# The ends of four layers: both products taken in two passes of 512 columns over the rows, with the gate weights split in between

## The reference

```
h = h + mixer(...) @ w_out            # block 2: h + rms_norm(mixer @ w_out, post_gain)
gate = sigmoid(h @ ple_gate[i])       # 1024 x 1024 weights
h = h + gate * (p[i] @ ple_proj[i])   # side input p: 1024 x 256
...
hn = rms_norm(h, next_gain)           # before the next layer
```

## Time and profile before

| | |
|---|---|
| median of three runs | 4260.09 us (4253.25, 4260.09, 4288.84) |
| profiled execution | 4255.36 us |
| its span | 4253.6 us |
| PE busy | 3758.1 us, 88% of the span |
| VectorE (DVE) busy | 2016.2 us, 47% |
| ScalarE (ACT) busy | 1703.1 us, 40% |
| DMA | 265.62 MB, mean 62 GB/s |
| landing of a 512 KB load of old h, median | 7.8 us after its issue |
| mean granted clock of TensorE | 0.91 of full speed |

### The profile page before, as it was taken

One profiled execution on the slowest core, in us unless ns is written; L12 is line 12 of the kernel. 1 busy time (PEld: TensorE's weight loads), 2 busy tenths in 40 slices (PEclk: granted clock), 3 DMA queues, 4 the chain that ended last, 5 costly groups with the idle time before them and its releaser, 6 DMA issues. The chain is left out here.

```text
span 4253.6 us, 48223 instructions
## 1 busy us (share of the span) xinstructions
PE 3758.1 (88%) x18866; PEld 3044.6 (72%) x18866; DVE 2016.2 (47%) x3934; ACT 1703.1 (40%) x3132; POOL 107.6 (3%) x120
## 2 busy tenths in 40 slices
PE   6999679889995999999788999999788999998789
PEld 5888337668883777777666777777676688877666
DVE  3143323354335667775334455555544355565441
ACT  3222461344332333342234444444433465655420
POOL 0011120000000000000000000000000000000000
PEclk9999799989995777788899999999898999999789
DMA  3333302212222121121321111010122111110310
GB/s 125 114 127 114 111 0 80 85 45 94 103 76 74 40 63 40 40 50 40 124 79 41 33 31 31 26 36 21 45 90 80 63 32 40 35 35 11 134 50 40
DMA packets 219642, 265.62 MB, mean 62 GB/s; under 512 B 62620, under 2 KB 142612, under 8 KB 218392
## 3 DMA queue, kind: packets, MB, share of 16 engines
q1 hardware_dynamic: 219416, 262.53, 18.9%
HBM read 191.95 MB, written 70.52 MB: 62 GB/s over the span
## 5 line engine op out<-in xcount | busy, mean ns | idle before, releaser
L320 PE MATMUL bank<-wh,XH 128*128 128x512 f32 x1344 | 556.1, 414 | 55.9 <-DVE wl L304 38.2
L320 PE MATMUL bank<-wh,XL 128*128 128x512 f32 x1344 | 530.3, 395 | 0.0
L320 PE MATMUL bank<-wl,XH 128*128 128x512 f32 x1344 | 530.0, 394 | 0.0
L2325 PE MATMUL bank<-XH,wh 128*128 128x512 f32 x1040 | 427.2, 411 | 32.1 <-DVE wl L2314 19.8
L2325 PE MATMUL bank<-XH,wl 128*128 128x512 f32 x1040 | 411.5, 396 | 0.0
L2325 PE MATMUL bank<-XL,wh 128*128 128x512 f32 x1040 | 410.7, 395 | 0.0
L320 PEld LDWEIGHTS bank<-wh,XH 128*128 128x128 f32 x1344 | 257.0, 191 | 126.0 <-issue 50.7
L304 DVE TENSOR_TENSOR wl<-raw,wh 128x1024 fp32r<-128x1024 f32 x128 | 155.6, 1235 | 312.8 <-ACT wh L295 311.6
L320 PEld LDWEIGHTS bank<-wh,XL 128*128 128x128 f32 x1344 | 257.4, 192 | 60.4 <-issue 10.0
L320 PEld LDWEIGHTS bank<-wl,XH 128*128 128x128 f32 x1344 | 256.5, 191 | 56.1
L320 PE MATMUL bank<-XH,wh 128*128 128x512 f32 x704 | 278.7, 396 | 5.9 <-DVE XL L1435 5.9
(11 more groups left out here) (401 smaller groups left out, 7367.2 us busy)
## 6 DMA issues: line engine op xcount, KB each, us to landing
sc_zt<-stage SPq DMA_DIRECT2D x88, 256.0 KB, 2.0
raw<-in_att_w_in SPq DMA_DIRECT2D x33, 512.0 KB, 4.2
raw<-in_even_w_in SPq DMA_DIRECT2D x32, 512.0 KB, 5.1
raw<-in_odd_w_in SPq DMA_DIRECT2D x32, 512.0 KB, 4.7
raw<-in_rec_w_in SPq DMA_DIRECT2D x32, 512.0 KB, 4.0
sc_h<-H SPq DMA_DIRECT2D x24, 512.0 KB, 2.6
H<-sc_h SPq DMA_DIRECT2D x24, 512.0 KB, 7.8
sc_z<-stage SPq DMA_DIRECT2D x40, 256.0 KB, 2.0
```

What stands on the lines that cost most here:

```text
L320: done = e.matmul(out, lhsT, rhs, start=k == 0 and j == 0, stop=k == NK - 1 and j == 2)
L2325: done = e.matmul(bank[:, :], x[:, k, :], y[:, k, ts], start=k == 0 and j == 0, stop=k == NK - 1 and j == 2)
```

## The change

Each end now goes through the rows in passes of one half each:

1. `w_out` half 0, all 8 row blocks; the transposes of the side input stand behind row blocks 0 and 1.
2. `w_out` half 1, all 8; behind row block s the transposes of row block s - 2 of `H`. ScalarE and VectorE split the gate weights of half 0 here, one part per row block.
3. Gate and side product of half 0; the transposes of row blocks 6 and 7 stand behind the first two gate tiles, and the gate weights of half 1 are split here.
4. Gate and side product of half 1; behind each, the norm and the transposes of the row block before, as before the change.

The whole side input is loaded first in the end, to `tmp` and the two `sg` buffers. In the third and fourth end half 0 of a product is kept in `H` (a new copy on VectorE, 8 per end), so the old h has no place in `H`; it comes row block by row block into `ng` and `tmp` by turns. The add is one instruction over 1024 columns, where it was two.

```diff
+        halves = [(s, half) for half in range(2) for s in range(NS)]
-        self.mm = Turns(range(6), [("w", *r) for r in rows] + [(x, *r) for r in rows for x in "gp"])
-        self.tb = Turns((6, 7), [("h", *r) for r in rows] + [("p", *r) for r in rows[:4]] + [("n", *r) for r in rows])
+        self.mm = Turns(range(6), [("w", *r) for r in halves] + [(x, *r) for r in halves for x in "gp"])
+        self.tb = Turns((6, 7), [("p", *r) for r in rows[:4]] + [("h", *r) for r in rows] + [("n", *r) for r in rows])
...
+    def sp_row(self, e, s):
+        if self.pg is None:
+            if self.mixed is not None:
+                e.wait_ge(*self.low.at("mixed", s))
+            dst = self.H[:, s, :]
+        else:
+            if s % 2:
+                wait_all(e, self.tmp_free(self.tmps.former["post", s]))
+            elif s:
+                e.wait_ge(*self.added.at(s - 2, 1))
+            dst = self.residual(s)[:, :]
+        e.dma_start(dst, self.h[s * P:(s + 1) * P, :]).then_inc(*self.row[s].up("in"))
...
+        e.dma_start(self.tmp[:, :].rearrange("p (a n) -> p a n", a=4),
+                    self.p[0:512, :].rearrange("(a p) n -> p a n", p=P)).then_inc(*self.side.up(0))
+        for q in range(2):
+            e.dma_start(self.sg[q][:, :].rearrange("p (a n) -> p a n", a=2),
+                        self.p[512 + 256 * q:768 + 256 * q, :].rearrange("(a p) n -> p a n", p=P)).then_inc(*self.side.up(1, q))
         if self.mixed is not None:
...
-        for s in range(NS):
-            if self.mixed is not None:
-                e.wait_ge(*self.low.at("mixed", s))
-            e.dma_start(self.H[:, s, :], self.h[s * P:(s + 1) * P, :]).then_inc(*self.row[s].up("in"))
         if self.pg is not None:
             e.dma_start(self.pg[:, :], row_of(self.post_gain).to_broadcast([P, D])).then_inc(*self.pgin.up())
+        for s in range(2 if self.pg is not None else NS):
+            self.sp_row(e, s)
         e.dma_start(self.pw[:, :, :], self.ple_w.rearrange("(a p) n -> p a n", p=P)).then_inc(*self.pwin.up())
-        for q in range(2):
-            wait_all(e, self.tmp_free(self.tmps.former["side", 0]) if q == 0 else [(self.turned, ("p", 0, 1))])
-            e.dma_start(self.tmp[:, :].rearrange("p (a n) -> p a n", a=4),
-                        self.p[512 * q:512 * (q + 1), :].rearrange("(a p) n -> p a n", p=P)).then_inc(*self.side.up(q))
         self.w.sp(e, 2)
+        if self.pg is not None:
+            for s in range(2, NS):
+                self.sp_row(e, s)
         self.w.sp(e, 3)
-        if self.ng is not None:
+        if self.next_gain is not None:
+            if self.pg is not None:
+                e.wait_ge(*self.added.at(NS - 2, 1))
             e.dma_start(self.ng[:, :], row_of(self.next_gain).to_broadcast([P, D])).then_inc(*self.ngin.up())
         if self.mg is not None:
             e.dma_start(self.mg[:, :], row_of(self.mid_gain).to_broadcast([P, D])).then_inc(*self.mgin.up())
...
+    def pe_side(self, e, q):
+
+        e.wait_ge(*(self.side.at(1, 1) if q else self.side.at(0)))
+        for k in range(2):
+            wait_all(e, self.tb_free(self.tb.former["p", q, k]))
+            bank = self.c.banks[self.tb["p", q, k]]
+            for a in range(4):
+                src = self.sg[a // 2][:, (a % 2) * 256 + k * P:(a % 2) * 256 + (k + 1) * P] if q else \
+                    self.tmp[:, a * 256 + k * P:a * 256 + (k + 1) * P]
+                done = e.transpose(bank[:, a * P:(a + 1) * P], src, self.c.ident[:, :])
+            done.then_inc(*self.turned.up("p", q, k))
+
...
+        for s in range(NS):
+            self.pe_out(e, s, 0, marks[s])
+            if s < 2:
+                self.pe_side(e, s)
+        for s in range(NS):
+            self.pe_out(e, s, 1, ())
+            if s >= 2:
+                e.wait_ge(*self.added.at(s - 2, 1))
+                self.pe_turn(e, "h", s - 2, self.H[:, s - 2, :])
+        for s in range(NS):
+            self.pe_gate(e, s, 0)
+            if s < 2:
+                e.wait_ge(*self.added.at(s + 6, 1))
+                self.pe_turn(e, "h", s + 6, self.H[:, s + 6, :])
+            self.pe_ple(e, s, 0)
...
+                self.pe_gate(e, s, 1)
+                self.pe_ple(e, s, 1)
+            if s > 0 and self.next_gain is not None:
                 e.wait_ge(*self.normed.at(s - 1))
                 self.pe_turn(e, "n", s - 1, self.tmp)
...
-        self.w.ac(e, 2)
-        self.w.ac(e, 3)
+        for s in range(NS):
+            if s < 2:
+                for k in range(2):
+                    e.wait_ge(*self.turned.at("p", s, k))
+                    e.activation(self.pT[:, k, 512 * s:512 * (s + 1)], c.banks[self.tb["p", s, k]][:, :], ACT.Copy) \
+                        .then_inc(*self.sided.up(s, k))
+            if self.pg is not None:
+                self.ac_post(e, s, 0)
+        for s in range(NS):
+            if s < 4:
+                self.w.ac_part(e, 2, s)
+            if self.pg is not None:
+                self.ac_post(e, s, 1)
+                self.ac_root(e, "post", s)
+            if s >= 2:
+                self.ac_high(e, "h", s - 2)
+        for s in range(NS):
+            if s < 2:
+                self.ac_high(e, "h", s + 6)
+            self.ac_gate(e, s, 0)
+            if s < 4:
+                self.w.ac_part(e, 3, s)
...
+    def ve_post(self, e, s):
+
+        inv = self.ve_rms(e, "post", s)
+        if s == 0:
+            e.wait_ge(*self.pgin.at())
+        e.scalar_tensor_tensor(out=self.H[:, s, 0:512], in0=self.H[:, s, 0:512], scalar=inv, in1=self.pg[:, 0:512],
+                               op0=ALU.mult, op1=ALU.mult).then_inc(*self.scaled.up(s, 0))
+        e.scalar_tensor_tensor(out=self.H[:, s, 512:1024], in0=self.c.banks[self.mm["w", s, 1]][:, :], scalar=inv,
+                               in1=self.pg[:, 512:1024], op0=ALU.mult, op1=ALU.mult).then_inc(*self.scaled.up(s, 1))
+        e.wait_ge(*self.row[s].at("in"))
+        e.wait_ge(*self.scaled.at(s, 1))
+        e.tensor_tensor(self.H[:, s, :], self.H[:, s, :], self.residual(s)[:, :], ALU.add).then_inc(*self.added.up(s, 1))
...
+        for s in range(NS):
+            if self.pg is None:
+                self.ve_add(e, s, 0)
+            else:
+                e.wait_ge(*self.tile.at(0, s))
+                e.tensor_copy(self.H[:, s, 0:512], c.banks[self.mm["w", s, 0]][:, :]).then_inc(*self.kept.up(s))
+        for s in range(NS):
+            if s < 4:
+                self.w.ve_part(e, 2, s)
+            if self.pg is None:
+                self.ve_add(e, s, 1)
+            else:
+                self.ve_post(e, s)
+            if s >= 2:
+                self.ve_low(e, "h", s - 2)
+        for s in range(NS):
+            if s < 2:
+                self.ve_low(e, "h", s + 6)
+            self.ve_gate(e, s, 0)
+            if s < 4:
+                self.w.ve_part(e, 3, s)
```

More of the change, by code:

```diff
@@ L407, in __init__ @@
             last += [("next", s)] if next_gain is not None else []
-        self.sts = Turns(self.st, uses + last)
-        self.tmps = Turns([self.tmp], uses + [("side", 0)] + last)
-        self.sgs = Turns(self.sg, uses + [("gate", *r) for r in rows])
+        post = post_gain is not None
+        self.sts = Turns(self.st, ([("post", s) for s in range(NS)] if post else []) + last)
+        self.tmps = Turns([self.tmp], [("side", 0)] + ([("post", s) for s in range(1, NS, 2)] if post else []) + last)
+        self.sgs = Turns(self.sg, ([("post", *r) for r in halves] if post else []) + [("gate", *r) for r in halves])
         self.marks = [[(self.low, ("n", s, 0)), (self.low, ("n", s, 1))] for s in range(NS)]
@@ L509, in pe @@
-        for q in range(2):
-            e.wait_ge(*self.side.at(q))
-            for k in range(2):
-                wait_all(e, self.tb_free(self.tb.former["p", q, k]))
-                bank = c.banks[self.tb["p", q, k]]
-                for a in range(4):
-                    done = e.transpose(bank[:, a * P:(a + 1) * P], self.tmp[:, a * 256 + k * P:a * 256 + (k + 1) * P],
-                                       c.ident[:, :])
-                done.then_inc(*self.turned.up("p", q, k))
+        for s in range(NS):
+            self.pe_out(e, s, 0, marks[s])
+            if s < 2:
+                self.pe_side(e, s)
@@ L580, in ve_rms, with ac_gate @@
         return st[:, 2:3]
+    def ac_gate(self, e, s, half):
+        e.wait_ge(*self.tile.at(2 + half, s))
+        wait_all(e, self.sg_free(self.sgs.former["gate", s, half]))
+        e.activation(self.sgs["gate", s, half][:, :], self.c.banks[self.mm["g", s, half]][:, :], ACT.Sigmoid) \
+            .then_inc(*self.gate.up(s, half))
     def ac(self, e, before):
@@ L590, in ac @@
         self.w.ac(e, 1)
-        for s in range(NS + 1):
-            if s < NS and self.pg is not None:
-                banks = [c.banks[self.mm["w", s, half]][:, :] for half in range(2)]
-                former = self.sgs.former["post", s]
```

(25 more changed lines are left out.)

160 lines of the change are left out of this document (61 added, 99 removed).

## The result

The changed kernel took 4194.26 us (median of 4 runs, 4188.82 to 4209.05), the kernel before, run beside it, 4269.48 (4 runs, 4253.25 to 4288.84). The ratio is 0.9831, with an interval of 0.9801 to 0.9861: faster by 1.7%. The profiled execution took 4190.46 us, with a span of 4188.7.

A forecast was written before the change was run, and what follows sets the result against it. PE was taken to set each layer end's pace, losing time at the seam between `w_out` and gate tiles. 92.5 - 6.9 - 8.6 = 77.0 us gained gave 4183, stated as 4180 us, range 4162 to 4212.

The forecast's parts named there:

- The seams: Between the last `w_out` tile and the gate tiles, four ends: PE's waits and slow clock go, 92.5 us back.
- 2.5 for `pT`: Pass 1: second side transposes wait for banks ScalarE empties late; 2.5 us for all four ends, 1.3 in the fourth.
- the side input's 4.4: Start of each end: 1 MB first in the DMA queue; 2.9 us in the second, 0.5 in each other.
- rival (d): Pass 2: transposes not covered, PE waits 4.22 us at all 32, 135 us lost, 4313 us; chance 0.04.
- The cover of pass 2 and of the gate weights: Passes 2 and 3: norm, add and weight splitting finish before PE asks for them; cost taken as 0.
- Rival (b): Starts of passes 3 and 4: weights still late, about 4 us at each of eight borders, 32 us, 4212; chance 0.09.
- Pass 1: First pass of each end: side input delays and waits for emptied banks cost 2.9 + 1.5 + 2.5 = 6.9 us.
- Pass 4: Second end: 9.3 us per row against PE's 8.07, 8.6 us in seven rows; first and third end fit.
- (a): Pass 4, second end: each 1.2 us gap drops the clock to 1.2 GHz, 12.6 us more, 4193; chance 0.08.
- (c): Pass 4: norm waits for the same row's sigmoid, adding 3.3 us to each chain, 4220 us; chance 0.05.
- (e): Better: the side input hides and the double norm keeps up, 92.5 less 2 to 6, 4168 us; chance 0.08.
- The total: Whole kernel: 77.0 us gained, 4183 us, stated as 4180; chance 0.66.

The follow-up runs named there:

- second pair of profiles: The kernel before and the changed kernel, both unchanged, profiled once more: 4267.04 us (one run) and 4187.34 us, ratio 0.9796.
- late_weights: Changed kernel with both slots of gate weights split in one go between passes 2 and 3, as before the change: 4225.17 us, ratio 0.9882.
- no_lag: Changed kernel with pass 2's transposes of row blocks 0 to 5 right behind their own tile, not two tiles later: 4292.43 us, ratio 1.0043.
- after_again: The changed kernel, unchanged, profiled and timed once more: 4187.34 us, ratio 0.9796.
- norm_order: Changed kernel; in pass 4 of the second end the first norm precedes the last row block's copies, its square writing to spent weights: 4183.05 us, one run.
- gate_between: side_later plus norm_order; in the second end's pass 4, next sigmoid between the norms, second square to spent weights, transposes two row blocks behind: 4174.12 us, ratio 0.9779.
- side_later: Changed kernel with the side input loaded behind the fourth weight part (second end: also `mixed`), its transposes behind row blocks 2 and 3: 4200.73 us, one run.

## Why the prediction was right, step by step

**The seams.** I forecast 92.5 us back at the seams, less 2.5 for `pT` and 8.6 in pass 4 of the second end, so 81.4 within the ends (the side input's 4.4 fall at their starts). The ends gave 77.0: by end 17.6, 11.4, 24.9 and 23.0, where the terms before the waits of `pT` were 18.6, 12.8, 26.9 and 25.5. The order of the four and the signs are right; each is 1.0 to 2.5 smaller. In the third 1.3 and in the fourth 2.6 of that are the waits of the list above; about 1 us in each of the first two has no bracket, and I leave it open. The second pair of profiles gives 18.0, 9.5, 25.3 and 23.0, so differences of 1 to 2 us in one end are not resolved. By the split above, 63.1 us of waits and 25.8 of busy time at the lower clock, the seams gave back some 89 where I had 92.5. Two readings of mine were off: 46.52 for the second seam should be 46.50, and in the third end not every row block's transposes wait 4.22; the three waits for `XL` there are 1.07, 4.22 and 2.85, so the 135 us of rival (d) was too high for its own source.

**The cover of pass 2 and of the gate weights.** Taken at nothing, and nothing stands there: no bracket over 0.3 us in passes 2 and 3 of any end. That the cover was needed is shown by late_weights (26.5 us) and no_lag (98.6). Rival (b), 32 us, was near the price of late_weights. The wait of rival (d) exists, 4.4 us at each of the six transposes of the third and fourth end that no_lag moved, but only with no lag, not with the lag of two.

**Pass 1.** For the side input in the second end I forecast 2.9 and 2.1 was measured; for the three others 0.5 each. Their first products wait as long as without the side input ahead (4.44 and 5.97 here, 4.44 and 5.96 with it later), so 0 there; but the load delayed the fourth weight part in the fourth end, and PE waited 2.60 for `wl` one tile later, of which 1.9 went when the side input came later. For `pT` I had 2.5 for all ends, 1.3 of it in the fourth; 1.32 was measured in the third and none in the fourth, where the wait for `wl` came first. With 2.1 + 2.6 + 1.3 = 6.0 against 6.9 the size is right, the places partly not. The places also change from one execution to the next: in after_again the fourth end waited 1.25 for `wl` and then 0.98 for `pT`, where I had put it, and the third end 0.73 for `pT`.

**Pass 4.** I forecast 9.3 us per row block in the second end, a wait of 1.2 in each and 8.6 in all; measured 9.35 (2281.69 to 2291.04), waits of 1.04 to 1.08 after one of 1.76, 8.1 in all. No wait in the first and third end until the last row, 4.90 as in the earlier trace rows. The sum set two paths side by side that met within 0.1 us: from the second root over the table load, the sigmoid and VectorE's two steps to 2315.5, and 1.70 behind the transposes to 2315.4. It did not say which of them closes the loop, and with the waits before me I took the second for the cause. norm_order showed that it is not: the transposes and copies can be taken off that path at no gain. Its rows show the first path closing, and gate_between, that opening it frees PE. So the first path carries the 9.3; that the second came to the same number was chance.
By the Trainium skill ("ScalarE: Activation LUTs", section on what ACT_TABLE_LOAD costs) each switch to the sigmoid would have taken an estimated 1.4 more. The rows do not agree: in norm_order the load starts at 2269.24 and takes 1.28, and the sigmoid starts at 2270.53, 0.01 behind its end; the row block takes 9.35 with both loads at 1.28.

**The rivals.** (a) fell: the windows view of the row blocks with seven waits of 1.04 to 1.76 has a clock of 1.00:

```profile
2215.00:2282.00 67.00, 58.88 (x251) 42.06 (x250) 39.32 (x68) 48.13 (x76) 0.00 (x0) 1.00 0.14 56
```

The transposes behind each wait take 1.09 instead of 1.04, and that is all. The Trainium skill ("TensorE: Matmul & The Clock Gate", section on the second failure mode) describes a kernel in which short idles between groups make the clock swing; gaps of this size did not do so here. (c) fell as a whole, since the first and third end keep pace; that the sigmoid stands in the norm's way was true in the second end and already inside its 9.3. (e) did not happen with the change: the second end's waits and the start's 2.1 us stayed. It came with gate_between, whose ends, 897.9, are 90.7 less than before.

**The total.** 77.0 forecast, 74.9 by the ends, 75.2 by the medians. In time, 4180 was forecast from the runs known then; the 4194.26 measured is 14 above it. Of that 9 is the other median of the kernel before (4269.48 for 4260.09), 2 is the gain, and 3 the rounding of the sum, 4183, down to 4180.

## What to carry to other kernels

Where one engine sets the pace, look for the places where its work of one kind runs out and that of the next is not ready, and mix the two. Here the passes give the transposes two tiles of cover and each slot of weights a whole pass, and the lag between making and using a tile is as much part of the change as the order. When an engine waits the same time in every row block, follow the work of one row block through the other engines until it comes back to its start: the loop may not contain the engine that waits, and then only what shortens or overlaps that loop helps. And where the unchanged parts vary by more than the effect (here by up to 28 us, against 6 for side_later and 9 for gate_between), measure the changed stretch by itself.

## What the runs showed of the hardware

- The rest of the span, whose instructions are the same in all nine kernels but for loads at the ends' starts, took 3265.0 to 3293.1 us: up to 28 us from one execution to the next, most of it between the first and second end (1161.0 to 1186.7). The sums of the ends of one kernel agree within 2.4.
- TensorE's granted clock stayed at 1.00, which is 2.4 GHz, through seven gaps of 1.04 to 1.76 us, one in each 9.35 us; in the third end of no_lag, with gaps of 4.42 or 4.43 us, one in each 12.4 to 13.6, it was 0.78 on average, and the transposes behind four of these five gaps took 1.97 instead of 1.03 (1.18 behind the other).
